# One product per chunk in the first branch's recurrence, with everything else formed for all chunks beforehand

## What is computed

```
def step(S, inp):
    r_t, k_t, v_t, w_t, kk_t, a_t = inp
    sa = jnp.einsum('bhvk,bhk->bhv', S, -kk_t)
    S = (S * w_t[:, :, None, :] + sa[..., :, None] * (kk_t * a_t)[..., None, :]
         + v_t[..., :, None] * k_t[..., None, :])
    return S, jnp.einsum('bhvk,bhk->bhv', S, r_t)
```

## Time and profile before

| | |
|---|---|
| Median of 3 runs | 2694.05 us (2692.04 to 2698.79) |
| The profiled execution's own time | 2693.0 us |
| Its span in the profile | 2691.2 us |
| PE busy | 2583.7 us, 96% of the span |
| POOL, DVE, ACT busy | 1391.5, 1308.5, 715.1 us (52%, 49%, 27%) |
| Granted TensorE clock, mean | 0.989 |

### The profile page before, as it was taken

One profiled execution on the slowest core, in us unless ns is written; L12 is line 12 of the kernel. 1 busy time (PEld: TensorE's weight loads), 2 busy tenths in 40 slices (PEclk: granted clock), 3 DMA queues, 4 the chain that ended last, 5 costly groups with the idle time before them and its releaser, 6 DMA issues.

```text
span 2691.2 us, 62636 instructions
## 1 busy us (share of the span) xinstructions
PE 2583.7 (96%) x25748; PEld 2462.3 (91%) x25748; DVE 1308.5 (49%) x1864; ACT 715.1 (27%) x1248; POOL 1391.5 (52%) x1187
## 2 busy tenths in 40 slices
PE   6999999999999999999999999999999999999996
PEld 6989889899899999999988998998988999999996
DVE  7534435345246633336673453453553566333455
ACT  4323323223224211112242232242232322111122
POOL 6435346254256655556762552543543566555565
PEclk9999999999999999999999999999999999999998
DMA  5112122022125422213421221221212362222122
GB/s 190 59 64 84 47 84 93 26 95 71 38 94 191 142 86 86 87 61 86 130 85 33 86 89 34 96 66 48 99 53 70 115 197 99 88 92 86 59 82 98
DMA packets 84682, 234.52 MB, mean 87 GB/s; under 512 B 12192, under 2 KB 16176, under 8 KB 83456
## 3 DMA queue, kind: packets, MB, share of 16 engines
q1 hardware_dynamic: 61632, 179.35, 21.2%
q10 hardware_dynamic: 19296, 39.66, 4.0%
q0 software_dynamic: 3552, 12.56, 1.4%
HBM read 199.55 MB, written 31.98 MB: 86 GB/s over the span
## 4 chain that ended last, share of the span: by engine, by line
PE 85%; DVE 4%; PEld 4%; ACT 3%; issue 2%; POOL 1%; DMA 1%; SPq 0%; ACTq 0%; PEldq 0%; DVEq 0%; POOLq 0%
PE psP L677 47%; PE psQ L677 15%; PE psQ L739 11%; PEld psP L677 3%; PE psQ L732 2%; PE psQ L1012 2%; PEld psQ L677 1%; PE psQ L985 1%; PE psP L1002 1%; PE psP L739 1%; DVE BIG L1675 1%; PE psQ L977 1%; PE psP L996 1%; PE psQ L935 1%; DVE BIGR L1564 1%
## 5 line engine op out<-in xcount | busy, mean ns | idle before, releaser
L520 POOL TENSOR_SCALAR WS<-W 128x512 fp32r<-128x512 f32 (+1 forms) x396 | 295.3, 746 | 734.4 <-PEq L671 426.3
L677 PE MATMUL psP<-HH,WS 128*128 128x272 f32 x2400 | 524.4, 304 | 10.5 <-issue 4.9
L677 PE MATMUL psP<-BIGR 128*128 128x272 f32 x3360 | 468.6, 290 | 4.7 <-PE psQ L677 3.3
L677 PE MATMUL psP<-HH,WR 128*128 128x272 f32 x2144 | 447.7, 291 | 0.0
L677 PE MATMUL psP<-HL,WS 128*128 128x272 f32 x2144 | 447.6, 291 | 0.0
L677 PEld LDWEIGHTS psP<-BIGR 128*128 128x128 f32 x3360 | 437.9, 189 | 9.4 <-issue 7.8
L522 POOL TENSOR_TENSOR WR<-W,WS 128x512 fp32r<-128x512 f32 x284 | 410.1, 1444 | 23.7
L677 PEld LDWEIGHTS psP<-HH,WS 128*128 128x128 f32 x2400 | 375.9, 190 | 27.9 <-issue 9.6
L677 PE MATMUL psQ<-BIGR,WS 128*128 128x272 f32 x2848 | 387.7, 288 | 1.5 <-DVE BIGR L1564 1.4
L677 PEld LDWEIGHTS psQ<-BIGR,WS 128*128 128x128 f32 x2848 | 367.7, 188 | 2.6 <-DVE BIGR L1564 1.9
L677 PEld LDWEIGHTS psP<-HL,WS 128*128 128x128 f32 x2144 | 341.3, 191 | 0.0
(11 more groups left out here) (297 smaller groups left out, 3374.0 us busy)
## 6 DMA issues: line engine op xcount, KB each, us to landing
W<-in_w_stage SPq DMA_DIRECT2D x88, 512.0 KB, 3.5
W<-in_w_f SPq DMA_DIRECT2D x88, 512.0 KB, 3.4
W<-in_w_gate SPq DMA_DIRECT2D x48, 512.0 KB, 3.9
W<-in_w_f SPq DMA_DIRECT2D x88, 256.0 KB, 2.6
gates_waiting<-GB ACTq DMA_DIRECT2D x48, 272.0 KB, 4.1
W<-in_w_br SPq DMA_DIRECT2D x48, 256.0 KB, 2.8
BIG<-gates_waiting ACTq DMA_DIRECT2D x36, 272.0 KB, 3.8
W<-in_w_out SPq DMA_DIRECT2D x16, 512.0 KB, 3.4
```

The lines of the kernel that those rows point to most:

```text
L520: pool.tensor_scalar(high, src, 1.0, 0.0, ALU.mult, ALU.add).then_inc(high_part[q], 1)
L677: mm = pe.matmul(out[:, a, 0:HT], a_, x_[:, a * HT:(a + 1) * HT], start=(first and n == 0), stop=(last and n == 2))
```

## The change

For a chunk with state S before it, U is TT (WV + WQ S) and the new state is a sum of products plus TK1 by U plus S. The change writes the chunk as one product: with QT, the product of TT and TK[0], it forms M = I + QT by TK[1] beforehand (**MT**), and the new state is M by S plus terms that do not hold S. The read-out takes the same road: QT by NR is added to AR, so that the output needs one product with S.

- The products AK by TK[3], which stood in WQ, move into the I1 jobs (9 pairs), and ACT copies them there in one or two more instructions per group (WV, WV8).
- After M4 comes `fill(18, 24)` in one piece, then **QU** (8 pairs for QT, 8 pairs TT[1] by WV for U without the state), **KS** (8 pairs TK[2] by TK[3]), the outputs' TK[3] by AK (8 pairs), a wait for U on ACT, TK[1] by U (8 pairs), **MA** (7 pairs QT by TK[1], 7 pairs QT by NR), U by NR (8 pairs), and XT.
- The chain then has, for the chunks 1 to 7, a wait for DVE's next state, MT by ST into KS, and the output's ST by AR. No fill stands in it. The samples' products stand in it instead: one pair and U8's two pairs, the first half of S8, and the sixteen 64x4 outputs, now alternating between the two halves of the partitions.
- Behind it come the second half of S8, `fill(24, 32)`, `value_tokens("C")`, `fill(32, 35)` and `fill(35, 39)`.
- UM and VM are formed by POOL instead of DVE: VM after the eighth split half of the fill tiles, UM after the ninth, behind a wait for U of the samples. UMV lies in NL4 now.
- ACT copies U and QT each in one 128x512 instruction in place of eight copies of U; it copies C3 and the third branch's values behind the first branch's output, not before it. DVE multiplies C2 before the chain and scales the state out of KS.
- Several semaphores are merged (C_k0 and C_f0 into C_f, A_n and A_y2 into A_o, and so on); the waits stay where they were. The small jobs behind M4 have places of their own in Q0 and Q1.

In all PE issues 96 products more than before (12 in each stage, 6 pairs).

```
@@ SMALL_A, CHAIN_A
+CHAIN_A = [("QU", "Q1"), ("KS", "Q0"), ("MA", "Q1"), ("S8", "Q1"), ("C_vt", "Q0"), ("A_mean", "Q1")]
@@ POOL
-                    split_fill(0, 12)
+                    split_fill(0, 8)
+                    wait_emptied(pool, l, ph, turn, "I32")
+                    wait_emptied(pool, l, ph, turn, "tok2")
+                    pool.tensor_tensor(blocks(VM, HD), bc(TK[:, 3, 8], 1, DEC_B), bc(K["maskb"][:], 2, HD), ALU.mult).then_inc(S["vm"], 1)
+                    split_fill(8, 9)
+                    pool.wait_ge(S["u8s"], it + 1)
+                    pool.tensor_tensor(blocks(UM, HD), bc(U[:, 8], 1, DEC_B), bc(K["maskb"][:], 2, HD), ALU.mult).then_inc(S["um"], 1)
+                    split_fill(9, 12)
@@ PE, in the I1 jobs
+                        after(f"tok{g}")
+                        for i in range(PER):
+                            c = PER * g + i
+                            mm = heads(b[:, 1, HD * i:HD * i + HD], AK[:, c, 0:HD], TK[:, 3, c])
@@ PE, the chain before
-                        b = job(f"U{c}")
-                        mm = heads(b[:, 0, 0:HD], TT[1][:, c], WQ[1][:, c], True, c == 0)
-                        if c:
-                            mm = heads(b[:, 0, 0:HD], WQ[0][:, c], ST[c % 2], False, True)
-                        filled(f"U{c}", mm)
-                        b = job(f"S{c}")
-                        heads(b[:, 0, 0:HD], TK[:, 2, c], TK[:, 3, c], True, False)
-                        if c:
-                            heads(b[:, 0, 0:HD], K["eye64"], ST[c % 2], False, False)
-                        fill(*((20 + c, 21 + c) if c < 4 else (0, 0)))
-                        after(f"U{c}")
-                        mm = heads(b[:, 0, 0:HD], TK[:, 1, c], U[:, c], False, True)
-                        filled(f"S{c}", mm)
...
@@ PE, the chain of the change
+                    pe.wait_ge(S["mt"], it1)
+                    for c in range(1, NC - 1):
+                        pe.wait_ge(S["s_next"], it * 7 + c)
+                        mm = heads(sums[c], MT[:, c], ST[c % 2], False, True)
+                        if c < NC - 2:
+                            mm.then_inc(S["s_sum"], 1)
+                        else:
+                            filled("KS", mm)
+                        if c == 1:
+                            after("MA")
+                        mm = heads(outs[c], ST[c % 2], AR[:, c, 1], False, True)
...
+                        elif c == 3:
+                            pe.wait_ge(S["vm"], it1)
+                            sb8 = job("S8")
+                            heads(sb8[:, 0], TK[:, 2, 8], VM, True, False)
...
+                    filled("A_out", mm)
+                    pe.wait_ge(S["um"], it1)
+                    filled("S8", heads(sb8[:, 0], TK[:, 1, 8], UM, False, True))
+                    fill(24, 32)
                     value_tokens("C", UC[:, 3 * TOK:])
+                    fill(32, 35)
@@ DVE
+                    dve.wait_ge(S["s_sum"], it * 7 + 1)
+                    next_state(0)
+                    b = filled("MA")
+                    tt(MT[:, 1:8], blocks(b[:, 0, HD:8 * HD], HD), bc(K["eye64"][:], 1, 7), ALU.add).then_inc(S["mt"], 1)
+                    emptied_by("MA", tt(AR[:, 1:8, 1], AR[:, 1:8, 1], blocks(b[:, 1, HD:8 * HD], HD), ALU.add))
+                    for c in range(1, 7):
+                        dve.wait_ge(S["s_sum"], it * 7 + c + 1)
+                        next_state(c)
```

More of the change, by code:

```diff
@@ L889, in stage @@
                             filled(f"M{step + 1}{g}", mm)
[L891 to L900, removed]
@@ new lines, in stage @@
+                    fill(18, 24)
+                    b = job("QU")
+                    for c in range(NC):
+                        after(f"M4{min(c // PER, 2)}")
+                        if c == NC - 1:
+                            heads(b[:, 0, HD * c - HD:HD * c], TK[:, 0, c], TT[1][:, c])
+                        elif c:
+                            heads(b[:, 0, HD * c - HD:HD * c], TT[1][:, c], TK[:, 0, c])
+                    for c in range(NC - 1):
+                        mm = heads(b[:, 1, HD * c:HD * c + HD], TT[1][:, c], WV[:, c])
@@ new lines, in stage @@
+                    filled("QU", mm)
+                    kb = job("KS")
+                    sums = [kb[:, 0, HD * c:HD * c + HD] for c in range(NC - 1)]
+                    for c in range(NC - 1):
+                        heads(sums[c], TK[:, 2, c], TK[:, 3, c], c == 0, False)
+                    ob = job("A_out")
+                    outs = [ob[:, 0, HD * c:HD * c + HD] for c in range(NC - 1)]
+                    for c in range(NC - 1):
+                        heads(outs[c], TK[:, 3, c], AK[:, c, HD:2 * HD], c == 0, False)
@@ L930, in stage @@
+                    filled("MA", mm)
+                    for c in range(NC - 1):
+                        heads(outs[c], U[:, c], NR[:, c, HD:2 * HD], False, c == 0)
                     pe.wait_ge(S["sdec"], it1)
-                    b = job("XT")
                     for h in range(2):
@@ L934, in stage @@
                         for s in range(DEC_B):
-                            mm = pe.matmul(b[q, 0, 4 * s:4 * s + 4], SD[q, HD * s:HD * s + HD], WQ[0][q, 8, 4 * s:4 * s + 4],
+                            mm = pe.matmul(kb[q, 1, 4 * s:4 * s + 4], SD[q, HD * s:HD * s + HD], QT[q, 8, 4 * s:4 * s + 4],
                                            start=True, stop=True, skip_group_check=True)
[L937 to L940, removed]
@@ L941, in stage @@
-                    heads(b[:, 0, 0:HD], TT[1][:, 8], WQ[1][:, 8], True, False)
-                    mm = heads(b[:, 0, 0:HD], XTB, K["eye64"], False, True)
-                    filled("U8", mm)
-                    value_tokens("C", UC[:, 3 * TOK:])
[L945 to L949, removed]
-                    heads(b[:, 0], TK[:, 1, 8], UM, True, False)
@@ L961, in stage, with sample_outputs @@
-                    filled("A_out", mm)
+                    mm.then_inc(S["xt"], 1)
+                    o8 = ob[:, 1, 0:HD]
+                    def sample_outputs(a, z):
+                        for s in range(a, z):
+                            for h in range(2):
+                                q = slice(HD * h, HD * h + HD)
+                                pe.matmul(ob[q, 1, 4 * s:4 * s + 4], SD[q, HD * s:HD * s + HD], AR[q, 8, 1, 4 * s:4 * s + 4],
+                                          start=False, stop=False, skip_group_check=True)
@@ L1295, in stage @@
                         b = wait_full(act, l, ph, turn, f"I1{g}")
-                        taken(f"I1{g}", NL2[:, c:c + PER], b[:, 0, 0:384].rearrange("p (a b d) -> p a b d", b=2, d=HD))
+                        act.activation(NL2[:, c:c + PER], b[:, 0, 0:384].rearrange("p (a b d) -> p a b d", b=2, d=HD), ACT.Copy)
+                        m = prompt_chunks(g)
+                        if m < PER:
+                            act.activation(WV8, b[:, 1, HD * m:HD * m + HD], ACT.Copy)
+                        taken(f"I1{g}", WV[:, c:c + m], blocks(b[:, 1, 0:HD * m], HD))
                     evacuate("C", 0)
```

172 lines of the change are left out of this document (84 added, 88 removed).

## The result

The changed kernel takes **2653.01 us** (median of 4 runs, 2647.51 to 2654.66) against 2694.41 us of the kernel before on the same chip: a ratio of 0.9844, 95% interval 0.9832 to 0.9856. It is faster by 1.6%. The forecast was 2660, with 2650 to 2667 as the range of the likeliest case alone.

A forecast was written before the change was run, and what follows sets the result against it. PE's list of work plus its waits bounds the kernel. Stretch terms sum to 30.6 us against 35.2, eight stages gain 37; 2693.0 - 37 + 3 = 2659, median 2660 us, range 2650 to 2667 (wider 2646 to 2678).

The forecast's parts named there:

- the likeliest case: The whole kernel: shorter stretches and two more clock falls give 2660 us, range 2650 to 2667; chance 0.62.
- The stretch: PE's work from step 18 to step 35 in one stage: 30.6 us, with I1's added pairs, against 35.2.
- I1: Jobs ahead of the stretch: 9 pairs move into them at 0.116 us each, 1.04 us on PE's path.
- the link: Chain, PE waiting for DVE's next state: bare 0.75 us for five of six links, bounded above by ACT's 0.85.
- C3's wait: Ahead of C's transposes: PE waits for ACT's copy of C3 out of PSUM, 0.86 us idle per stage.
- 0.19 us at its edges: Each block of fill between pairs: 0.19 us on top of 0.75 a step; two blocks pay, 0.38 us.
- 4.9 us: Old stretches other than stage 8: their excess from PE stops and one clock fall, assumed to remain.
- +3 us: Chain behind XT: two more clock falls than before, +3 us; the ends were none (0) and one per stage (12 us).
- rival 1: The clock falls in every stage's chain, behind XT's low work: 2667 us; chance 0.18.
- 4 (the chain at half clock): Clock stays at 1.2 GHz from QU to S8's end: 10.8 us more per stage, 2743 us; chance 0.04.
- 2 (stops for instructions): Dense pairs and chain: PE stops for its instructions, two more of 0.93 us per stage, 2675 us; chance 0.10.
- 3 (a wait at UM or C3 beyond the forecast): POOL in mid-split when U8 arrives delays UM: PE waits some 0.9 us more per stage, 2667 us; chance 0.06.

The follow-up runs named there:

- e_oldbare: The kernel before, its fill steps 19 to 23 in one block ahead of the chain and 24 to 31 in one behind it: 2705.6 us, ratio 1.0045.
- after_again: The changed kernel run again as it is, as measure for other runs on the same chip: 2657.6 us, ratio 0.9855.
- e_pairs: The changed kernel with six read-out pairs (chunks 5, 6, 7) moved into the links of chunks 4, 5 and 6: 2650.4 us, ratio 0.9832.
- e_umdve: The changed kernel with UM and VM formed on DVE again, UM behind the state's output: 2667.1 us, ratio 0.9901.
- e_xt: The changed kernel with XT's loops exchanged, so its products alternate between the two halves of the array: 2646.0 us, ratio 0.9813.
- e_edges: The changed kernel with fill steps 18 to 23 cut into six single steps among QU's pairs: 2670.2 us, ratio 0.9911.
- e_link: The changed kernel with one more DVE copy of 128x64 ahead of the scaling in each of six links: 2665.3 us, ratio 0.9897.

## Why the prediction was right

*The stretch.* Forecast 30.6 less the 1.04 of I1, about 29.6; measured 29.36 to 29.38. Part by part: 62 pairs 7.2 (7.28), XT 1.8 (about 1.6), the link 0.75 (0.72) and 1.1 at chunk 3 (1.10), S8's second half 0.98 (0.95), C3's wait 0.86 (from 348.03 + 0.25, where step 31 ends, to 349.15: 0.87), I1 1.04 (0.92), UM on POOL 1.28 (1.04). The choice of the lower bound for the link, 0.75 and not ACT's 0.85, held. No wait came at U, MT or UM.

*What was mis-sized.* Three terms.
- "0.19 us at its edges" is 0.34 a block. The sum hardly felt it, because with three blocks left the end that was not counted is small; the sum for e_oldbare, with more blocks, did.
- The "4.9 us" of stops and one fall in the old stretches, "left standing": all gone, the eight stretches are equal. This is most of why 2653 is below 2660. The fill between the old links is not needed for them: e_oldbare has none there, and more stops. What in the old chain does stays open, and the profile names no releaser for them.
- "+3 us" for the clock in the chain: there is no fall in any of the eight stretches of this trace, and one, of 1.3 us, in after_again. The falls of this trace came later, in work that the change doesn't touch: 2.8 us more in the windows from A_mean to C_var, out of the 5.4 that were given back in all (45.7 less 40.3). That the term looks right in the sum is luck.

So the likeliest case was right in its mechanism, 37 us against 39.9 for the clean stages (8 x 5.86 less 7.0). The forecast still lies 7 us above the median, chiefly because the old stops went too.

*The rivals.* 1 (a fall in every chain) and 4 (the chain at half clock): in this trace the clock is 1.00 in all stretches (the earlier trace rows showed a fall to 0.50 before). But the place that the prediction named is one of falls. The same kernel run again, after_again, has one in stage 1: its windows with XT, and behind it in the chain, are

```profile
149.50:152.90 3.40, 3.40 (x92) 3.34 (x88) 1.42 (x4) 0.20 (x1) 0.00 (x0) 1.00 0.00 0
152.90:156.30 3.40, 3.40 (x40) 2.11 (x36) 0.57 (x2) 0.22 (x1) 1.04 (x1) 0.50 0.02 5
```

and e_pairs has one in four of its eight chains. So rival 1 came true in some chains of some traces, in no trace in every chain. The Trainium skill's page "TensorE: Matmul & The Clock Gate" (Part 1) says that idleness takes the clock away. In this trace the chain, with its idle links, kept it, and ahead of a fall the records, whose ends are modelled, show PE busy for the whole window, as in the earlier trace rows; the idleness that the prediction saw in that fall is not in the rows. Two windows of the changed kernel, stage 1, in and behind eight products of 128x4 (sixteen records) of another branch:

```profile
193.30:196.70 3.40, 3.40 (x31) 3.24 (x29) 1.55 (x2) 0.69 (x2) 2.87 (x4) 1.00 0.29 116
196.70:200.10 3.40, 3.40 (x18) 3.40 (x17) 1.50 (x4) 0.00 (x0) 1.35 (x2) 0.51 0.12 43
```

2 (stops for instructions): none in the eight stretches. 3 (a wait at UM or C3 beyond the forecast): UM was two microseconds early; e_umdve shows what it would have cost, 1.02 us a stage.

*What the gain is.* Outside the 17 steps the stretch of stage 8 took 22.5 us before (35.22 - 12.75) and 16.6 after. Before, S8 and the sample outputs stood alone at its end, here in PE's timeline of stage 8:

```profile
2057.22 1.94 PE L739 MATMUL psQ<-BIG 64*64 64x512 f32 x8
...
2059.22 1.77 PE L959 MATMUL psP<-BIG,SD 64*64 64x4 f32 x32
2060.92 0.52 PE L677 MATMUL psP<-HH,WS 128*128 128x272 f32 x2
```

Old chain 12.7, WQ 2.6, S8 2.0 (with the pair behind it), sample outputs 1.7 and U8 0.4, one behind the other, 19.4 in all, became 7.3 of pairs and 5.9 of chain with the samples' work in its links and S8's second half behind it, 13.2. The new wait for C3, 0.87, takes part of these 6.2 us back; what is left over to 5.9, 0.5 us, lies in XT and in edges. So it is the algebra that shortens the chain, by these parts; the moved fill alone made the kernel slower. The merged semaphores and the joined copies of ACT were not run alone, but the parts add up without a term for them.

## What to carry to other kernels

Fill between the links of a dependent chain is no free cover: count its edges, at both ends, against the waiting that it hides; in the old chain they were equal, in the new one the edge cost twice what the fill hid, and only a shorter chain helped. Small products of the same kind fit into the idle time of a link without any edge, and gave nearly their full time. When a wait is to be covered, look for everybody who waits for the same copy (here the next job on the same PSUM buffer), and measure a stage where the clock is whole rather than a median that carries falls of the clock.

## What the runs showed of the hardware

- Sixteen products of 64x4 that alternate between the two halves of the array take 0.91 us, eight of one half and then eight of the other about 1.6 (e_xt and the changed kernel). The Trainium skill's page "TensorE: Matmul & The Clock Gate" (Part 3, packing small matmuls) says that products on distinct row groups run side by side. The trace of e_xt agrees: a product of one half starts within 0.01 us of that of the other.
- A block of 128x128 steps between runs of 64x64 pairs costs 0.34 us more than the same products in two runs (five more blocks, 1.72 us in e_edges), 0.19 of it seen in the step and 0.15 in the pairs.
- Two DVE instructions on 128x64 with no wait between them start 0.14 us apart though the first lasts 0.23 (e_link).
- The clock fell to its lower level, 1.2 GHz, behind eight products of 128x4 (1.00 and then 0.51 in the windows of the changed kernel) and behind XT (1.00 and then 0.50 in after_again), with PE busy by its records in the windows ahead of the falls; in which stages it did so changed from run to run of one kernel.
